# Splitting the experts' first products into three one-pass products, with loads and key-making moved between engines

## The reference, cut to what matters

```python
def one(xc):
    ...
    ids = ...                      # 128 expert ids of each token
    g = softmax(best)              # and their weights
    ue, ve = u[ids], v[ids]
    a = gelu(einsum('cd,chkd->chk', xc, ue))
    return einsum('chk,chkd->cd', g * a, ve)
```

## Time and profile before

| | us |
|---|---|
| median of 3 runs | 3880.26 |
| lowest, highest | 3876.89, 3895.60 |
| the profiled execution | 3902.94 |
| its span | 3901.1 |

### The profile page before, as it was taken

The page is one execution under the profiler, slowest core; times in us unless marked ns, Lnnn a source line. Parts: engine busy times, 40 slices in busy tenths (PEclk is TensorE's granted clock), DMA queues, the critical chain, the costliest instruction groups (busy, mean ns, idle before and its releaser), DMA issues. The chain is left out here.

```text
span 3901.1 us, 39658 instructions
## 1 busy us (share of the span) xinstructions
PE 3270.2 (84%) x14052; PEld 2358.8 (60%) x14052; DVE 2204.2 (57%) x3970; ACT 890.2 (23%) x1338; POOL 934.0 (24%) x757
## 2 busy tenths in 40 slices
PE   6789879987968978989498898453599999999997
PEld 4645558875844656868277645342466666666664
DVE  3136433355315534337563432798977888777766
ACT  2134333312214323321223333210110000000001
POOL 0021100000002100000001110001778666777653
PEclk9868889998976988999698969776599999999998
DMA  3420022253430012334135001112489999999996
GB/s 122 135 74 1 22 70 97 91 180 109 139 105 22 1 43 92 97 122 174 42 118 143 14 21 66 39 38 82 140 317 363 373 366 367 357 365 366 402 409 252
DMA packets 206520, 617.92 MB, mean 158 GB/s; under 512 B 31472, under 2 KB 65040, under 8 KB 200720
## 3 DMA queue, kind: packets, MB, share of 16 engines
q1 hardware_dynamic: 132624, 347.28, 25.6%
q0 software_dynamic: 73728, 268.47, 18.5%
HBM read 596.92 MB, written 18.74 MB: 158 GB/s over the span
## 5 line engine op out<-in xcount | busy, mean ns | idle before, releaser
L109 PE MATMUL psum<-sbuf 128*128 128x512 f32 (+1 forms) x1680 | 679.2, 404 | 251.3 <-DVE sbuf L1861 99.0
L110 PE MATMUL psum<-sbuf 128*128 128x512 f32 (+1 forms) x1680 | 663.5, 395 | 0.0
L111 PE MATMUL psum<-sbuf 128*128 128x512 f32 (+1 forms) x1680 | 662.3, 394 | 0.0
L109 PEld LDWEIGHTS psum<-sbuf 128*128 128x128 f32 x1680 | 324.6, 193 | 334.6 <-DVE sbuf L1861 101.0
L2099 PE MATMUL psum<-sbuf 128*128 128x512 f32 x1024 | 472.6, 604 | 5.6 <-DVE sbuf L2227 5.6
L2090 PE MATMUL psum<-sbuf 128*128 128x256 f32 x2048 | 465.3, 380 | 0.0
L2090 PEld LDWEIGHTS psum<-sbuf 128*128 128x128 f32 x2048 | 390.6, 191 | 107.2 <-issue 60.3
L1153 POOL TENSOR_TENSOR sbuf<-sbuf 64x768 fp32r<-64x768 f32 (+2 forms) x22 | 29.2, 1329 | 1743.7 <-ACT sbuf L1099 1743.7
L2052 POOL DMA_INDIRECT sbuf<-peer_u,sbuf x256 | 373.4, 1459 | 84.0 <-issue 52.2
L110 PEld LDWEIGHTS psum<-sbuf 128*128 128x128 f32 x1680 | 325.1, 193 | 70.2 <-issue 5.0
L111 PEld LDWEIGHTS psum<-sbuf 128*128 128x128 f32 x1680 | 323.9, 193 | 68.3
(11 more groups left out here) (272 smaller groups left out, 4539.8 us busy)
## 6 DMA issues: line engine op xcount, KB each, us to landing
sbuf<-peer_ut SPq DMA_DIRECT2D x128, 512.0 KB
sbuf<-peer_v SPq DMA_DIRECT2D x128, 512.0 KB
sbuf<-w_ffn SPq DMA_DIRECT2D x88, 512.0 KB, 3.4
sbuf<-w_mod SPq DMA_DIRECT2D x24, 1024.0 KB, 5.1
sbuf<-w_down SPq DMA_DIRECT2D x16, 1408.0 KB, 6.0
sbuf<-w_fm SPq DMA_DIRECT2D x38, 512.0 KB, 4.4
sbuf<-w_out SPq DMA_DIRECT2D x24, 512.0 KB, 3.5
sbuf<-w_tm SPq DMA_DIRECT2D x10, 1024.0 KB, 5.8
```

The lines of the kernel that those rows point to most:

```text
L109: nc.tensor.matmul(acc, w_high(k), x_high(k), start=(k == 0), stop=False)
L110: nc.tensor.matmul(acc, w_high(k), x_low(k), start=False, stop=False)
L111: mm = nc.tensor.matmul(acc, w_low(k), x_high(k), start=False, stop=(k == kt - 1))
```

## The change

Three things are moved at once.

1. **`up` in three one-pass products.** The tokens are split once (`h_high`, `h_low`), `u` in every slot: ScalarE copies 128 x 1024 to `u_high`, VectorE subtracts to `u_low`, and TensorE runs `split_products`, 24 matmuls of 256 columns in place of 16. The splits of slots 0 and 1 stand in the opening at groups 8 and 16, that of slot `s + 2` stands behind slot `s`'s gelu on ScalarE and behind its gate multiply on VectorE.
2. **`u`'s loads three slots ahead.** SP starts `u(s + 3)` right after `v(s)`, and its place is free when the low part of `u(s)` is made.
3. **One-hot keys on ScalarE.** All groups from 32 on and the odd ones before get their 128 x 1024 one-hot from ScalarE: 8 squares of 128 columns and one `Relu(1 - x)` over 1024. VectorE keeps the even groups below 32, and `equal` of all.

To make room the ring of rows now lies in `xT` and `hT`: `xT` is stored to memory first (2 MB) and loaded back at the end, and gathers wait for the store.

```diff
+    h_dense = hT[:, :, tok0:S]
+    rows = [(xT, hT)[r // 4][:, r % 4 * 2:r % 4 * 2 + 2, :].rearrange("p k s -> p (k s)") for r in range(RING)]
...
+    def on_act(n):
+        return n >= GROUPS or n % 2 == 1
+    def squares(n):
+        return sum(map(on_act, range(n)))
...
-        rows, odd = sb([P, RING, D]), sb([P, D])
+        odd = sb([P, D])
+        u_high, u_low = sb([P, 2, D], F32R), sb([P, 2, D], F32R)
+        h_high, h_low = sb([P, KT, DENSE], F32R), sb([P, KT, DENSE], F32R)
...
+            def load_u(s):
+                if s >= HELD:
+                    sp.wait_ge(u_low_made, s - HELD + 1)
+                sp.dma_start(u_in[:, s % HELD, :], ut[s]).then_inc(u_landed[s % HELD], 16)
+            sp.dma_start(x_d, xT[:, :, :].rearrange("p k s -> p (k s)")).then_inc(x_stored, 16)
+            for s in range(HELD):
+                load_u(s)
             for s in range(NKEY):
-                if s >= HELD:
-                    sp.wait_ge(a_made, s - HELD + 1)
-                sp.dma_start(u_in[:, s % HELD, :], ut[s]).then_inc(u_landed[s % HELD], 16)
                 if s >= HELD:
                     sp.wait_ge(y_made, s - HELD + 1)
                 sp.dma_start(v_in[:, s % HELD, :], v[s * P:(s + 1) * P, :]).then_inc(v_landed[s % HELD], 16)
+                if s + HELD < NKEY:
+                    load_u(s + HELD)
+            sp.wait_ge(x_stored, 16)
+            for n in range(ROWS - RING, ROWS - RING // 2):
+                wait_row(sp, n)
+            sp.dma_start(xT[:, :, :].rearrange("p k s -> p (k s)"), x_d).then_inc(x_back, 16)
+            sp.wait_ge(x_back, 16)
...
-                pool.wait_ge(hot_made, 2 * n + 2)
+                pool.wait_ge(equal_made, n + 1)
...
+                    elif n < RING // 2:
+                        pool.wait_ge(x_stored, 16)
+                    else:
+                        pool.wait_ge(h_low_made, 1)
+                    pool.indirect_dma_start(rows[n % RING], None, (u, v)[f],
...
-                pe.wait_ge(hot_made, 2 * n + 2)
+                if on_act(n):
+                    pe.wait_ge(one_made, squares(n) + 1)
+                else:
+                    pe.wait_ge(own_made, n - squares(n) + 1)
...
+                    pe.wait_ge(h_low_made, 1)
                 else:
                     pe.wait_ge(gelu_done, s - 1)
-                pe.wait_ge(u_landed[s % HELD], 16 * (s // HELD + 1))
-                for k in range(KT):
-                    mm = nc.tensor.matmul(a_ps[:, s % 2, 0:DENSE], u_in[:, s % HELD, k * P:(k + 1) * P], hT[:, k, tok0:S],
-                                          start=(k == 0), stop=(k == KT - 1))
-                mm.then_inc(a_made, 1)
+                pe.wait_ge(u_low_made, s + 1)
+                split_products(nc, a_ps[:, s % 2, 0:DENSE], KT, lambda k: u_high[:, s % 2, k * P:(k + 1) * P],
+                               lambda k: u_low[:, s % 2, k * P:(k + 1) * P], lambda k: h_high[:, k, :],
+                               lambda k: h_low[:, k, :]).then_inc(a_made, 1)
...
+            nc.scalar.activation(h_high[:, :, :], h_dense, ACT.Copy).then_inc(h_high_made, 1)
+            def split_u(s):
+                act.wait_ge(u_landed[s % HELD], 16 * (s // HELD + 1))
+                nc.scalar.activation(u_high[:, s % 2, :], u_in[:, s % HELD, :], ACT.Copy).then_inc(u_high_made, 1)
+            def one_hot(n):
+                if n >= 2:
+                    act.wait_ge(gates_made, n - 1)
+                for j in range(GROUP):
+                    at = n % GROUPS * GROUP + j
+                    nc.scalar.activation(hot[:, n % 2, j, :], C.iota[:, :], ACT.Square, bias=picked[:, 1, at:at + 1],
+                                         scale=-1.0).then_inc(squared, 1)
+                act.wait_ge(squared, GROUP * (squares(n) + 1))
+                nc.scalar.activation(hot[:, n % 2, :, :], hot[:, n % 2, :, :].bitcast(F32), ACT.Relu, bias=C.ones[:, 0:1],
+                                     scale=-1.0).then_inc(one_made, 1)
...
+            one_hot(1)
             for n in range(GROUPS):
+                if n in (8, 16):
+                    split_u(n // 8 - 1)
                 take(n)
                 gelu_dots(n - GROUPS)
+                if n + 2 < GROUPS and on_act(n):
+                    one_hot(n + 2)
             for s in range(NKEY):
+                if s + GROUPS < QUARTERS * GROUPS and on_act(s + GROUPS):
+                    one_hot(s + GROUPS)
                 act.wait_ge(a_made, s + 1)
                 if s >= 2:
                     act.wait_ge(w_made, s - 1)
                 nc.scalar.activation(act_out[:, s % 2, :], a_ps[:, s % 2, 0:DENSE], ACT.Gelu).then_inc(gelu_done, 1)
+                if s + 2 < NKEY:
+                    split_u(s + 2)
...
-                if n >= 2:
-                    dve.wait_ge(gates_made, n - 1)
                 toks = slice(g * GROUP, (g + 1) * GROUP)
-                nc.vector.tensor_tensor(hot[:, n % 2, :, :], C.iota[:, :].unsqueeze(1).to_broadcast([P, GROUP, NKEY]),
-                                        picked[:, 1, toks].unsqueeze(2).to_broadcast([P, GROUP, NKEY]),
-                                        ALU.is_equal).then_inc(hot_made, 1)
+                if not on_act(n):
+                    if n >= 2:
+                        dve.wait_ge(gates_made, n - 1)
+                    nc.vector.tensor_tensor(hot[:, n % 2, :, :], C.iota[:, :].unsqueeze(1).to_broadcast([P, GROUP, NKEY]),
+                                            picked[:, 1, toks].unsqueeze(2).to_broadcast([P, GROUP, NKEY]),
+                                            ALU.is_equal).then_inc(own_made, 1)
...
+            def split_u(s):
+                dve.wait_ge(u_high_made, s + 1)
+                if s >= 2:
+                    dve.wait_ge(a_made, s - 1)
+                nc.vector.tensor_tensor(u_low[:, s % 2, :], u_in[:, s % HELD, :], u_high[:, s % 2, :].bitcast(F32),
+                                        ALU.subtract).then_inc(u_low_made, 1)
             dve.wait_ge(copied, 2)
+            dve.wait_ge(h_high_made, 1)
+            nc.vector.tensor_tensor(h_low[:, :, :], h_dense, h_high[:, :, :].bitcast(F32), ALU.subtract).then_inc(h_low_made, 1)
             for n in range(GROUPS):
+                if n in (8, 16):
+                    split_u(n // 8 - 1)
...
                 nc.vector.tensor_tensor(w[:, s % 3, :], gate[:, q % 2, s % QUARTER, :], act_out[:, s % 2, :],
                                         ALU.mult).then_inc(w_made, 1)
+                if s + 2 < NKEY:
+                    split_u(s + 2)
                 use_rows(s)
```

More of the change, by code:

```diff
@@ L1964, with peer_experts @@
 GROUP = 8
-def peer_experts(nc, C, hT, h_tok, stream, ids, weights, ut, u, v, u_in, y):
+def peer_experts(nc, C, xT, hT, h_tok, stream, ids, weights, ut, u, v, u_in, y, x_d):
     DENSE = (ST - GT) * P
@@ L2009, in peer_experts @@
         v_landed = [sem.one(f"v_landed{r}") for r in range(HELD)]
-        turned, copied, high_made, low_made, hot_made, parts_made, gates_begun, gates_made, gates_taken, a_made, gelu_done, w_made, y_made = [sem.one(x) for x in (
-            "picks_turned", "picks_copied", "high_made", "low_made", "hot_made", "parts_made", "gates_begun", "gates_made", "gates_taken", "a_made", "gelu_done", "w_made", "y_made")]
+        turned, copied, high_made, low_made, one_made, equal_made, parts_made, gates_begun, gates_made, gates_taken, a_made, gelu_done, w_made, y_made = [sem.one(x) for x in (
+            "picks_turned", "picks_copied", "high_made", "low_made", "one_made", "equal_made", "parts_made", "gates_begun", "gates_made", "gates_taken", "a_made", "gelu_done", "w_made", "y_made")]
+        x_stored, x_back, u_high_made, u_low_made, h_high_made, h_low_made, squared = [sem.one(x) for x in (
+            "x_stored", "x_back", "u_high_made", "u_low_made", "h_high_made", "h_low_made", "squared")]
+        own_made = sem.one("own_made")
         dots_gelu, dots_weighed, summed, y_taken = [sem.one(x) for x in ("dots_gelu", "dots_weighed", "summed", "y_taken")]
@@ L2051, in fetch_rows @@
                         wait_row(pool, n - RING)
-                    pool.indirect_dma_start(rows[:, n % RING, :], None, (u, v)[f],
+                    elif n < RING // 2:
[3 more added lines that the diff above has]
+                    pool.indirect_dma_start(rows[n % RING], None, (u, v)[f],
                                             bass.IndirectOffsetOnAxis(ap=stream[:, t, j:j + 1], axis=0)
@@ L2168, in one_hot @@
                                         picked[:, 0, toks].unsqueeze(2).to_broadcast([P, GROUP, QUARTER]),
[L2169 removed]
+                                        ALU.is_equal).then_inc(equal_made, 1)
             def take(n):
@@ L2191, in use_row @@
                 if f == 0:
-                    nc.vector.tensor_tensor_reduce(out=rows[:, r, :], in0=rows[:, r, :], in1=h_tok[:, t, :], scale=1.0,
+                    nc.vector.tensor_tensor_reduce(out=rows[r], in0=rows[r], in1=h_tok[:, t, :], scale=1.0,
```

(7 more changed lines are left out.)

1 line of the change is left out of this document (removed).

## The result

The changed kernel takes 3951.78 us (median of 4 runs, 3948.79 to 3959.70). The kernel before takes 3887.93 beside it (4 runs, 3876.89 to 3900.90). The ratio is 1.0166, with a 95% interval of 1.0126 to 1.0206: slower by 1.7%, 64 us. The forecast was 3896 us with a range of 3856 to 3922. It was wrong.

What follows compares the result with a forecast made beforehand. The bound was taken to be a two-slot loop through VectorE, GpSimd and TensorE. Terms 4.5 - 10 + 13 + 6 + 1 + 1 + 1 = +16.5 us, put on the median 3880.3, gave 3896 us; range 3856 to 3922.

Steps and rivals of the forecast that it cites:

- With 7.3 of 8.3 us at work I take it to stay at 1.00: Slots with groups: TensorE's granted clock stays at 1.00, the full 2.4 GHz, with the shorter `up`.
- loop sum: Two slots with groups, through VectorE, GpSimd and TensorE: 16.48 us with rows of `v`, for 16.43 before; 16.64 with `u`.
- TensorE waiting near 1 us ahead of each group: Sign that the forecast is right: TensorE waits near 1 us before each group's products.
- The clock: Rival: clock falls with TensorE's longer idle pieces, tens of us per tenth of slots at 0.50; 0.07 with other mishaps.
- GpSimd's pace: Rival: the new subtraction delays another gather, 8.5 us a slot with rows of `u`; 3908 or 3917 us; chance 0.13.
- the term of +6: The 60 slots with rows of `u`: GpSimd's late gathers and multiply, between -6 and +12 us, taken as +6.
- the 0.9 "by that page": GpSimd's gathers in slots with rows of `u`: 0.9 us each by the skill page, making that term -6 us.
- TensorE's pace: Rival: the loop has slack, each slot with groups falls by the whole 0.58 us, 3836 us; chance 0.14.
- The opening: Before the slots: pairs 6.85 us for 7.52, saving 10 us; two waits for ScalarE's high part of 6.3, +13 us.
- the start of the layer: Ahead of the first one-hot: two new steps over 2048 columns, copies and subtractions, +4.5 us.
- Slots 96 to 127: Slots without groups: transfers hold the pace at 7.39 us a slot, the shorter `up` buys nothing, +1 us.
- The end: After the last rows: `xT` comes back, 5 us of transfer and some latency beside the last 6 us of work, +1.

Runs made afterwards that it cites:

- the longer loop: The kernel before, float32 products, with VectorE making the one-hot of each group of slots 0 to 95 twice; 3968.15 us, ratio 1.0203.
- the products alone: The changed kernel with all one-hots back on VectorE, early loads and moved ring kept; 4089.01 us, ratio 1.0498.
- the ten matmuls: The changed kernel with ten unused 256-column matmuls on TensorE between `up` and the group in even slots; 3923.67 us, ratio 1.0103.
- the keys alone: The kernel before with only the one-hots moved to ScalarE (all groups from 32 on, odd ones before); 3840.55 us, ratio 0.9874.
- Loads alone: The kernel before with only the loads of `u` started three slots ahead, right behind `v`; 3890.30 us, ratio 1.0015.
- five: The changed kernel with five unused 256-column matmuls on TensorE between `up` and the group in even slots; 3934.75 us, ratio 1.0117.

## Why the prediction was wrong

**The step that failed** is one sentence: "With 7.3 of 8.3 us at work I take it to stay at 1.00." I judged the clock by TensorE's mean share of work, and the trace of before gave me only a kernel whose idle pieces are short (0.65 ahead of the group in the earlier trace rows). My own loop sum said that they would get longer: `up` is 0.58 shorter, the one loop as long as before, so TensorE's idle time in two slots grows by 2 x 0.58 = 1.16 us, all in the one place where it waits. 0.65 + 1.16 = 1.81, and the trace has 1.84. The prediction had put "TensorE waiting near 1 us ahead of each group"; it is twice that, ahead of every second one. The clock was among the rivals, at 0.07 together with other mishaps, priced by tens of us for each tenth of the slots and without a sum of its own; its price was up to 102 / 2 = 51 us, and the range left out the worst of it.

The Trainium skill (TensorE: Matmul & The Clock Gate, Terms) puts the cost of time under the throttle at that time multiplied by the share of pulses held back, here half. This case agrees roughly: 51 of 102 us by that rule, beside a stage that is 847.9 - 802.6 = 45 us longer than the same loop without the falls, and 25.6 of 51 beside 80 - 55 = 25 in the kernel before with the longer loop. With the products alone it is too much, 147 by the rule beside 124, so it is an upper end.

**The loop was right.** Pairs of slots without a fall take 16.47 us where rows of `v` are used and 16.62 where those of `u` are, for 16.48 and 16.64 forecast. VectorE does wait for the high part, 0.5 us at a time, in the odd slots, whose rows the loop runs through:

```profile
DVE sbuf L2278 <- ACT sbuf L2162: 21.3, 43, 0.5
```

That is a row of the waits in the slots with groups: line that waits, line waited for, total, times, longest. In the earlier trace rows VectorE went from the gate multiply to the rows without such a wait. What the shorter `up` gave, this wait took back, as forecast. One thing was not in the sum: in most even slots the gate multiply L2302 starts while GpSimd is at work and takes 1.22 us (rows of `v`) or 1.58 (rows of `u`), not 0.42, and the subtraction follows without a wait. It didn't lengthen the loop, which doesn't pass through the rows of the even slots.

**GpSimd's pace** was not reached. The slots with rows of `u` took 8.20 us each before, and 16.62 for two now is 0.1 a slot more, as the term of +6 had it; the rival's 8.5 us a slot did not come. With the ten matmuls in place it is 8.40 to 8.45 a slot there and 8.23 as before with rows of `v`, which is why that stage is 10 us longer than before and not 7. The prediction read the Trainium skill (SBUF — State Buffer, Who interferes with whom) too narrowly at this point: a gather's row names SBUF among what it reads (`sbuf<-peer_u,sbuf` in the earlier trace rows), so the rule that it quotes first, two SBUF inputs against an instruction that reads SBUF, may cover the gathers, and the 0.9 "by that page" does not follow. The sum went by the 1.99 of the trace and does not hang on it.

**TensorE's pace**, the faster rival, did not come in this kernel, and came in another: with the keys alone the loop drops below TensorE's work and the slots run at 7.84.

**The opening** was right in its parts: pairs take 6.77 us for 6.85 forecast, the two stalls 7.0 each for 6.3 (a distance of 11.16 for 4.16), the start of the layer 3.9 (first `equal` at 7.16 us for 3.25) for 4.5.

**Slots 96 to 127** stayed with the transfers, 409 GB/s as 408 before. They run at 7.07 us a slot, before at 7.12: the forecast's 7.39 was too long for both, and right in that nothing changes. The end, with `xT` coming back, cost TensorE 1.4 us (its last wait ahead of the transposes is 5.03 us, before 3.60), for 1 forecast.

**The parts do not add up**, and that is the main thing that the experiments add. Keys alone: 3841, about -53 against the kernel before. Loads alone: no difference. Products with the early loads and the moved ring: 4089, about +195. Together: +64, and not 195 - 53 = 142. The keys take the same 1.14 us out of the loop in both cases, but beside the products they also bring the time at 0.50 from 294 to 102 us. The products had no gain to give as long as the loop held the pace. One call moved out of the loop (the low part ahead of the gate multiply) turns the same set of edits from 1.7% slower to 0.7% faster, and 1.3% with the low parts of the opening moved too. That is where the keys alone are as well (ratios 0.9871 and 0.9874): the split products, well placed, added nothing that can be measured. What moving the ring costs by itself was not run.

## What to carry to other kernels

When a change shortens work on TensorE but not the loop that TensorE waits in, add up its idle piece after the change, where it falls, and not only its mean share of work: here, with 0.65 us once in two slots, the clock stayed at 1.00 but for one fall, and with 1.84 us in the same place it fell 22 times and cost 45 to 51 us. Cost the clock as a rival with a sum: the microseconds at the low level, halved, as the upper end. Ask of an operation that you add whether it stands on the chain between two engines' waits: the low part of `u` there and ahead of the gate multiply is one moved call and 87 us. And count what it meets in its new place: the same subtraction took 1.22 us in the one and 2.27 on average in the other.

## What the runs showed of the hardware

- Falls of the clock by the idle pieces of TensorE in 94 slots, median piece and falls: 0.58 us, 1 fall; 0.81 us (ten matmuls filled in), 1; 1.29 us (five), 15; 1.71 us (float32 products, longer loop), 14; 1.84 us, 22; 2.78 us, 45. The other five versions have 0 to 2 falls, with medians of 0.57 to 0.81 us. TensorE was busy 95% of the slots' time with the ten matmuls in place (clock 1.00), 92% with five (0.97), 90% with the longer float32 loop (0.97), 89% in the kernel after (0.94) and 86% with the products alone (0.85). The runs don't separate the length of a piece from the share of work, since one loop sets both, nor either of them fully from the form of the products.
- Equal idle pieces of 1.84 us, one after another, were followed by a fall in some cases and not in others, as in the two groups shown above.
- A two-input subtraction of VectorE over 1024 columns took 1.21 to 1.23 us in the kernel after. Started during a GpSimd multiply of 1.05 us it took 2.02, and started during a gather 2.4 to 2.7 in 54 of 59 cases (the run with the low part moved).
- Runs of one kernel differ as the clock does. With the loads alone, the fastest run (3883.08 us) had a mean granted clock of 0.887 and the slowest (3908.18) of 0.881. What that lacks to 1.00, times the span, is 439 and 465 us, 26 more for 25 us more of time; with the low part moved it is 27 more for 28. These totals don't show which causes which. Ahead of the layer, from 2248 to 2310, the trace does: TensorE is busy for 60 us in both profiled executions, with 119 matmuls at a clock of 0.50 before and 177 at 0.83 after.
